# The first pair of modulation blocks of a fused decoder trunk, moved from VectorE sums to TensorE row products

## What is computed

```python
c_act = jax.nn.silu(c)
for i in range(DEPTH):
    mod = c_act @ ada_w[i] + ada_b[i]          # (2048) @ (2048, 12288)
    sh1, sc1, g1, sh2, sc2, g2 = jnp.split(mod, 6, axis=-1)
    h = x * (1.0 + sc1) + sh1
    y = mixer(h)                               # layer 0: gated DeltaNet beside S5; layer 1: conv beside attention
    x = layer_norm(ALPHA * x + (1.0 + g1) * y, ...)
    h = x * (1.0 + sc2) + sh2
    x = layer_norm(ALPHA * x + (1.0 + g2) * swiglu(h), ...)
```

## Time and profile before

| | us |
|---|---|
| runs | 2762.1, 2764.23, 2772.07 |
| median of the three | 2764.23 |
| the profiled execution, its own time | 2765.13 |
| its span, first to last instruction | 2763.5 |
| PE busy in the span | 2552.3 |
| DVE busy | 2036.5 |
| ACT busy | 1219.4 |
| mean granted clock of TensorE, as a share | 0.953 |

### The profile page before, as it was taken

One profiled execution on the slowest core, in us unless ns is written; L12 is line 12 of the kernel. 1 busy time (PEld: TensorE's weight loads), 2 busy tenths in 40 slices (PEclk: granted clock), 3 DMA queues, 4 the chain that ended last, 5 costly groups with the idle time before them and its releaser, 6 DMA issues.

```text
span 2763.5 us, 41958 instructions
## 1 busy us (share of the span) xinstructions
PE 2552.3 (92%) x16596; PEld 2304.1 (83%) x16596; DVE 2036.5 (74%) x2454; ACT 1219.4 (44%) x1614; POOL 187.5 (7%) x226
## 2 busy tenths in 40 slices
PE   1499999888889999999999899998999999999998
PEld 1488888777878899889988799998878998899887
DVE  8879999878587777777778888568877655554556
ACT  1255556543454434443343453553454334443444
POOL 0012221000000000000001011000000000000000
PEclk8589999888999999999999899999999999999998
DMA  9874444555448778888878499456578655555552
GB/s 374 286 248 142 154 156 153 199 179 200 137 153 292 273 274 281 281 275 277 280 275 294 152 330 349 158 169 227 184 270 276 214 197 185 192 187 184 197 183 77
DMA packets 272987, 616.02 MB, mean 223 GB/s; under 512 B 23211, under 2 KB 23746, under 8 KB 272578
## 3 DMA queue, kind: packets, MB, share of 16 engines
q1 hardware_dynamic: 240020, 488.00, 52.1%
q0 software_dynamic: 32640, 125.84, 13.1%
q10 hardware_dynamic: 174, 0.04, 0.0%
HBM read 611.73 MB, written 2.10 MB: 222 GB/s over the span
## 4 chain that ended last, share of the span: by engine, by line
PE 79%; DVE 11%; DMA 3%; issue 2%; ACT 2%; SPq 2%; DVEq 0%; POOL 0%; POOLq 0%; ACTq 0%
PE groups L2539 12%; PE groups L2531 11%; PE groups L2543 11%; PE groups L2541 11%; PE groups L2535 11%; PE groups L2533 11%; DMA ada_units<-in_ada_w_dram 3%; PE pc L2710 2%; DVE ada_acc L2033 2%; SPq L1660 1%; PE pb L2700 1%; DVE w_lo L2051 1%; DVE ada_acc L2358 1%; PE groups L1132 1%; DVE xT L2171 1%
## 5 line engine op out<-in xcount | busy, mean ns | idle before, releaser
L1750 ACT ACTIVATE w_hi<-w_raw 128x1024 fp32r<-128x1024 f32 x776 | 817.2, 1059 | 1133.5 <-PE groups L2535 545.9
L2051 DVE TENSOR_TENSOR w_lo<-w_raw,w_hi 128x1024 fp32r<-128x1024 f32 x747 | 905.7, 1223 | 531.3 <-ACT w_hi L1750 527.4
L2531 PE MATMUL groups<-w_hi,act_hi 128*128 128x512 f32 x1408 | 554.2, 394 | 19.9 <-DVE act_lo L2185 19.9
L2535 PE MATMUL groups<-w_lo,act_hi 128*128 128x512 f32 x1408 | 550.5, 391 | 0.0
L2533 PE MATMUL groups<-w_hi,act_lo 128*128 128x512 f32 x1408 | 550.3, 391 | 0.0
L2539 PE MATMUL groups<-act_hi,w_hi 128*128 128x256 f32 x1776 | 510.9, 288 | 34.4 <-DVE act_lo L2185 14.2
L2541 PE MATMUL groups<-act_lo,w_hi 128*128 128x256 f32 x1776 | 502.6, 283 | 0.0
L2543 PE MATMUL groups<-act_hi,w_lo 128*128 128x256 f32 x1776 | 502.0, 283 | 0.0
L2539 PE MATMUL groups<-hid_hi,w_hi 128*128 128x256 f32 x1392 | 390.4, 280 | 0.0
L2541 PE MATMUL groups<-hid_lo,w_hi 128*128 128x256 f32 x1392 | 388.7, 279 | 0.0
L2543 PE MATMUL groups<-hid_hi,w_lo 128*128 128x256 f32 x1392 | 388.7, 279 | 0.0
(11 more groups left out here) (436 smaller groups left out, 2487.1 us busy)
## 6 DMA issues: line engine op xcount, KB each, us to landing
ada_units<-in_ada_w_dram POOLq DMA_DIRECT2D x120, 1024.0 KB, 6.6
w_raw<-in_ffn_w_gate_dram SPq DMA_DIRECT2D x88, 1024.0 KB, 5.2
w_raw<-in_ffn_w_up_dram SPq DMA_DIRECT2D x88, 1024.0 KB, 5.3
w_raw<-in_ffn_w_down_dram SPq DMA_DIRECT2D x88, 1024.0 KB, 5.2
w_raw<-in_cd_w_in_dram SPq DMA_DIRECT2D x48, 1024.0 KB, 5.3
w_raw<-in_ab_w_in_dram SPq DMA_DIRECT2D x40, 1024.0 KB, 5.9
ada_units<-in_ada_w_dram SPq DMA_DIRECT2D x80, 512.0 KB, 4.2
w_raw<-in_ab_w_out_dram SPq DMA_DIRECT2D x16, 1024.0 KB, 6.2
```

The source lines that it names most:

```text
L1750: act.activation(whi[:, half, k], raw[:, slot, k], ACT.Copy).then_inc(hi_done, 1)
L2051: dve.tensor_tensor(wlo[:, half, k], raw[:, slot, k], whi[:, half, k].bitcast(F32), ALU.subtract).then_inc(lo_done, 1)
L2531: pe.matmul(dst, hi[:, k, rows], whi[:, j % 2, kk], start=(k == 0), stop=False, skip_group_check=True)
L2535: last = pe.matmul(dst, hi[:, k, rows], wlo[:, j % 2, kk], start=False, stop=(k == UK * p["units"] - 1), skip_group_check=True)
```

## The change

`ada_op` no longer stands behind any n of `in0`. In its place PE does `ada_rows` behind the 48 matmuls of n = 3, 6, 9, ..., 24, ahead of `s5_out(n)`. One `ada_rows` takes two slots of `ada_units` as they are, as moving operand, with a column of `c_act` repeated 32 times as stationary operand: four products of 512 columns, of which each is written to its own 32 partitions of the bank `pm`, and over the eight groups each is accumulated there. Every one of 32 partitions then holds the same row. `ada_row_copy` on ACT copies `pm` into `ada_acc`, and `ada_sum(0)` turns the rows into eight columns of `pm`: eight products of two columns with columns of the identity, as many as before. Loads 4 to 15 are queued in pairs behind weight units 9, 12, ..., 24. The semaphore `dn_ada_dve` is renamed to `dn_ada_used` and now counts PE's groups by two for the first pair. The four other pairs stay on DVE.

```diff
-        EARLY_AT = (4, 5, 7, 11, 12, 13, 15, 19, 20, 21, 23, 27, 28, 29, 30, 31)
+        EARLY_ROWS = range(3, 27, 3)
...
-            if n - 4 in EARLY_AT[:12]:
-                deltanet_ada_load(sp, EARLY_AT.index(n - 4) + 4)
+            if n - 6 in EARLY_ROWS[:6]:
+                for a in range(2):
+                    deltanet_ada_load(sp, 2 * (EARLY_ROWS.index(n - 6) + 2) + a)
...
             act.wait_ge(dnd_set.sem, dnd_set.at(0, "hb"))
             squares(0)
             side_split(0)
+            ada_row_copy(act)
             rows_g(0)
...
+        def ada_rows(pe, pair_of_slots):
+
+            first, last_pair = pair_of_slots == 0, pair_of_slots == KT // 2 - 1
+            if first:
+                pe.wait_ge(mod_taken, glu["ab1"] + 1)
+            for a in range(2):
+                m = 2 * pair_of_slots + a
+                pe.wait_ge(dn_ada_in[m % 4], 16 * (m // 4 + 1))
+                for half in range(2):
+                    rows = slice(64 * a + 32 * half, 64 * a + 32 * half + 32)
+                    last = pe.matmul(pm[rows], cact[:, m:m + 1].broadcast_to([P, 32]),
+                                     ada_slot(m)[:, GROUP * half:GROUP * half + GROUP], start=first, stop=last_pair)
+            last.then_inc(dn_ada_used, 2)
+
+        def ada_row_copy(act):
+            act.wait_ge(dn_ada_used, KT)
+            act.activation(acc[:, 0], pm[:], ACT.Copy).then_inc(dn_row_taken, 1)
...
         def deltanet_early_dve(dve, n):
-            if n in EARLY_AT:
-                ada_op(dve, EARLY_AT.index(n))
...
             def ada_sum(pair):
-                if pair:
-                    on(dnd, f"take{pair - 1}")
-                else:
-                    pe.wait_ge(mod_taken, glu["ab1"] + 1)
-                pe.wait_ge(dn_ada_dve, KT * (pair + 1))
+                if pair == 0:
+                    pe.wait_ge(dn_row_taken, 1)
+                    for t in range(GT):
+                        for a in range(2):
+                            last = pe.matmul(pm[:, t:2 * GT:GT], acc[:, 0, P * t:P * t + P], ident[:, 64 * a:64 * a + 64:32],
+                                             start=(a == 0), stop=(a == 1), skip_group_check=True)
+                    done(last, f"ada{pair}")
+                    return
+                on(dnd, f"take{pair - 1}")
+                pe.wait_ge(dn_ada_used, KT * (pair + 1))
...
             def s5_after(i, j):
                 n = 8 * i + j
+                if n in EARLY_ROWS:
+                    ada_rows(pe, EARLY_ROWS.index(n))
                 s5_out(n)
```

More of the change, by code:

```diff
@@ L402, in build @@
         dn_ada_in = [sem(f"dn_ada_in{n}") for n in range(4)]
-        dn_ada_dve = sem("dn_ada_dve")
+        dn_ada_used, dn_row_taken = sem("dn_ada_used"), sem("dn_row_taken")
         level_masks = sem("dn_level_masks")
@@ L570, in deltanet_ada_load @@
             if m > 3:
-                sp.wait_ge(dn_ada_dve, m - 3)
+                sp.wait_ge(dn_ada_used, m - 3)
             rows, block = P * (m % 16), glu["ab1"] + 2 * (m // 16)
@@ L871, in ada_op @@
             else:
-                dve.wait_ge(dn_ada_dve, n)
+                dve.wait_ge(dn_ada_used, n)
                 last = dve.scalar_tensor_tensor(total, unit, cact[:, k:k + 1], total, ALU.mult, ALU.add)
-            last.then_inc(dn_ada_dve, 1)
+            last.then_inc(dn_ada_used, 1)
+        def ada_rows(pe, pair_of_slots):
[13 more added lines that the diff above has]
+            act.activation(acc[:, 0], pm[:], ACT.Copy).then_inc(dn_row_taken, 1)
         def deltanet_early_dve(dve, n):
-            if n in EARLY_AT:
-                ada_op(dve, EARLY_AT.index(n))
             if n in CONV_AT:
```

## The result

| | before | after |
|---|---|---|
| median, us (12 runs each) | 2765.05 | 2777.55 |
| lowest to highest | 2755.3 to 2772.07 | 2774.8 to 2779.96 |
| span of the profiled execution | 2763.5 | 2774.7 |

The ratio is 1.0048, with a 95% interval of 1.0036 to 1.0059: slower by 10 to 16 us, about 13, where +16 was forecast and 2780 us named. The bound of 0.5% (13.8 us) lies inside the interval, so "slower by over 0.5%", which the prediction held at 0.64, is neither shown nor excluded. The sum was close; two of its terms were wrong, in opposite directions, so part of that closeness is luck.

The account below looks back on a forecast made before the run. PE was taken to set the pace of `in0`, with DVE close behind. Eight groups at 17.2 us less a gain of 1.1 made +16.1 us, so the median 2764.2 became 2780 us, range 2768 to 2792.

Parts of the forecast that it names:

- slower by over 0.5%: Whole kernel: the time rises by more than the 13.8 us a measurement can tell from no change; chance 0.64.
- PE is the pace of `in0`, DVE is not: In `in0`: PE is busy throughout at 8.55 us a unit, so twelve of sixteen removed `ada_op` are worth nothing.
- Rival 3: In `in0`: DVE was the hidden bound, so its relief shortens units; -5 us, 2759 us; chance 0.03.
- the price of a group: On PE in `in0`: strips overlap by one record only, 2.15 us a group, 17.2 us for eight.
- the prediction's own test: Prediction wrong if a group costs under 1.9 or over 2.5 us, other units change, or `glu` waits as before.
- Rival 2: PE's groups in `in0`: all four strips run together, 0.86 us a group, 6.9 for eight, 2770.0 us; chance 0.25.
- a gain of 1.1 us: Behind `in0`: `ada_sum(0)` starts at 472.9 instead of 474.03, held by ACT's copy; bounds 0 to 2.1 us.
- so I count nothing: Behind 461.6: 1.7 us of lost clock may return with a shorter pause, but PE would only reach the copy sooner.
- Rival 4: At `ada_sum(0)`: ACT does not move up, the copy becomes the wait, 0.9 us late, 2782 us; chance 0.05.
- nothing for the loads and SP's queue: Loads in `in0`: SP does not stall and loads land in time, cost nothing; uncovered, up to 4.2 us each.
- A little off: Sum over partitions at `ada_sum(0)`: eight products, 1.68 us, taken as unchanged, between no gain and a loss of 0.1 us.
- the in-order mechanism: PE's groups: records begin in program order, adjacent strips overlap by one record; 2777 to 2784 us, likeliest at 0.37.

## Why the prediction came out as it did

**Right: PE is the pace of `in0`, DVE is not.** Fifteen ops less on DVE left every unit at 8.55 us, and the 8.6 us that the groups added to PE's `in0` came through in full. Rival 3 falls.

**Wrong: the price of a group**, "Between: PE's records begin in order in all rows I read ... 5 steps of 0.43 = 2.15 us, 17.2 us for eight". Eight groups cost 8.6 us, half of it, and by the prediction's own test (a price under 1.9 us a group) this step failed. A strip's second record does not hold back the records of other strips: the four first ones run together, and two strips in two orders cost the same. Rival 2, held at 0.25, had the mechanism, at 0.86 us; the measured 1.07 is that plus some 0.2 us in the unit behind, whose cause I did not find. The forecast that the units without a group stay at 8.55 us holds but for those right behind one, at 8.75. The Trainium skill, "TensorE: Matmul & The Clock Gate", Part 3 (Packing small matmuls), says that products to different strips run at the same time, and the runs agree: 0.87 us for four products, against 3.42 in one strip where `s5_out` shares it. Its rule that matmuls start in program order does not fit the starts seen with all products in one strip: `s5_out`, queued behind the group, begins at 222.12, ahead of records of the group at 222.54 and 222.97. The 1.45 us a group that the prediction estimated from the page's figure was 1.07.

**Wrong: "a gain of 1.1 us" behind `in0`.** It became a loss of 2.1 us. The steps up to it held: `s5_low` shows a wait of 1.3 us (forecast 1.2), the copy took 0.57 us (0.69), and `ada_sum(0)` starts 1.3 us earlier (1.1). What failed is "so I count nothing" for the clock. With the shorter pause the clock did not fall, which is why the removal gains 3.5 us where the copy is out of the way, instead of 2.1; and just because of it PE ran the four sides faster and came to the copy 2.25 us early instead of 1.0. Behind that second pause the clock did fall, for 3.4 us, and the copy's place cost 5.6 us. Rival 4 named the copy, but as a late ACT, with no clock in it.

**Right, as measured: nothing for the loads and SP's queue.** No wait of PE for `ada_units` shows in `in0`, though between 170 and 470 us those loads landed 6.6 us after their issue (median), not 4.2. **A little off:** `ada_sum(0)` costs more only through the clock; its sixteen records take 1.84 us in the same view in all kernels that have the full clock there.

**The sum.** Forecast 17.2 - 1.1 = 16.1; in the profile 8.6 + 2.1 = 10.7. The two errors are -8.6 and +3.2 us. That 2777.55 falls in 2777 to 2784, the range of the in-order mechanism, is luck: that mechanism is excluded, and without the second error the sum with the measured price would have been 2764.2 + 8.6 - 1.1 = 2771.7 us. The ratio says 10 to 16 us, so the profile's 10.7 lies inside; what the medians have above it, about 2 us, is not placed, and stretches with unchanged work move by as much between two profiles of one kernel.

## What to carry to other kernels

Where an engine is busy for all of a stretch, ask of added work only what it runs beside: the same 32 products cost 18 us in one strip, 8.6 us in four and 0.2 us when they leave free the strip that the next product needs. A producer placed just ahead of its consumer, because the engine "has nothing to do there", can cost more than its wait: price the clock behind the pause from a row that has one, and ask whether a pause that gets shorter in one place opens another further down. And look at the cheapest form of the gain first: what this change freed on DVE mattered only in the last two units, and one changed list of positions took the same 3.5 us of the stretch with no work on PE at all, though in the ratios, 0.9988 and 0.9992, so small a gain is barely clear of noise.

## What the runs showed of the hardware that was not expected

- Products in 32-bit floats with 32 stationary columns, written to different strips of 32 partitions, each follow their own order: four strips of two records ran in 1.06 us, two strips of four records in 1.7 us in either order, and three strips ran at once with products of two different lines and of 512 and 256 columns.
- Behind a group over all four strips, the 48 matmuls of the next unit began 0.118 us apart instead of 0.113, at a granted clock of 1.00; behind groups over two strips they kept 0.113.
- `s5_out` overtook a group in a single strip only from the group's fifth record on (222.12 against 220.37 us), so a long queue in one strip still delays what comes behind it.
- Pauses of PE of 1.3 us left the granted clock at 1.00 in the stretches shown; pauses of 2.1 to 2.2 us, which began 5.7 to 5.9 us behind the end of one of 1.3, left 0.56 to 0.78 of it over the 7.8 us behind them, and the kernel before had 0.86 over the 12.4 us from `s5_out(31)` to the sum, with its pause of 3.29 us in them.
